# Attention of block 1 and mix of block 2 written as straight lists in a new order

## The reference

```python
# block 1, the attention half of a layer
h = rms_norm(x, ln_attn_g[i])
dq, dk, dv, mq, mk, mv = jnp.split(h @ w_in[i], cuts, axis=-1)
# diff_attention: 4 heads with two maps each, softmax of q k^T * scale + bias(distance), causal
a = p[:, 0] - lam * p[:, 1]
out = rms_norm(einsum('bhqk,bkhe->bqhe', a, v), sub_g) * (1.0 - lam_init)
# moba_attention: 8 heads of 64, one block of 256 keys: plain causal softmax with bias
x = x + jnp.concatenate([y_diff, y_moba], axis=-1) @ w_out[i]

# block 2, the mix of a layer, between two SwiGLU halves
h = rms_norm_2(x, mix_norm[l])
q, k, v, f_logit, xr, gr, g_attn, g_rnn = jnp.split(h @ w_in[l] + b_in[l], SPLIT_POINTS, axis=-1)
c = jnp.cumsum(jax.nn.log_sigmoid(f_logit), axis=1)      # 8 heads
s = einsum('bhqd,bhkd->bhqk', q, k) * scale + (c_i[..., :, None] - c[:, :, None, :])
y_attn = (softmax(where(mask, s, -inf)) @ v) @ w_o_attn[l]
yr = rg_lru(causal_depthwise_conv(xr), ...) * jax.nn.gelu(gr)
merged = jax.nn.sigmoid(g_attn) * y_attn + jax.nn.sigmoid(g_rnn) * (yr @ w_o_rnn[l])
x = x + merged @ w_out[l]
```

## Time and profile before

| | |
|---|---|
| median of 3 runs | 2027.01 us |
| profiled execution, its own time | 2026.93 us |
| its span | 2025.1 us |
| TensorE matmuls busy | 1923.7 us (95%) |
| VectorE, ScalarE busy | 1204.7 us (59%), 1108.7 us (55%) |
| GpSimd busy | 39.9 us (2%) |
| mean granted TensorE clock | 0.979 of full |
| HBM read | 335.09 MB, 166 GB/s |

### The profile page before, as it was taken

One profiled execution on the slowest core, in us unless ns is written; L12 is line 12 of the kernel. 1 busy time (PEld: TensorE's weight loads), 2 busy tenths in 40 slices (PEclk: granted clock), 3 DMA queues, 4 the chain that ended last, 5 costly groups with the idle time before them and its releaser, 6 DMA issues.

```text
span 2025.1 us, 23105 instructions
## 1 busy us (share of the span) xinstructions
PE 1923.7 (95%) x9234; PEld 1600.6 (79%) x9234; DVE 1204.7 (59%) x1746; ACT 1108.7 (55%) x1588; POOL 39.9 (2%) x70
## 2 busy tenths in 40 slices
PE   6969999987999999999989999999999998999999
PEld 5757888765888888887778878888888877887888
DVE  5655776665776654545865655455455577565544
ACT  5745655664655554447865454445444686545442
POOL 2000000000000000000010000000000001000000
PEclk8989999999999999999999999999999999999999
DMA  7424455534554555553354655555555344455552
GB/s 240 146 83 146 167 187 185 166 128 125 166 189 170 183 187 188 187 166 125 130 178 137 218 176 188 191 178 186 187 187 172 123 142 167 139 192 167 187 187 104
DMA packets 156533, 337.65 MB, mean 167 GB/s; under 512 B 5798, under 2 KB 18555, under 8 KB 155915
## 3 DMA queue, kind: packets, MB, share of 16 engines
q1 hardware_dynamic: 153920, 327.57, 48.6%
q0 software_dynamic: 2048, 8.41, 1.4%
q10 hardware_dynamic: 459, 0.20, 0.0%
HBM read 335.09 MB, written 1.07 MB: 166 GB/s over the span
## 4 chain that ended last, share of the span: by engine, by line
PE 79%; DVE 10%; ACT 8%; issue 2%; DMA 1%; POOL 0%; SPq 0%; DVEq 0%; ACTq 0%; POOLq 0%
PE bank L408 24%; PE bank L410 24%; PE bank L409 24%; DVE w_lo L1396 4%; ACT w_hi L932 2%; ACT tmp L1084 1%; PE bank L569 1%; PE bank L523 1%; PE bank L477 1%; DMA raw<-in_w_in 1%; PE bank L658 1%; DVE gss L1571 1%; PE bank L702 1%; DVE tmp L1596 1%; ACT L1084 1%
## 5 line engine op out<-in xcount | busy, mean ns | idle before, releaser
L1396 DVE TENSOR_TENSOR w_lo<-raw,w_hi 128x1024 fp32r<-128x1024 f32 x620 | 733.4, 1221 | 385.5 <-ACT w_hi L932 378.7
L932 ACT ACTIVATE w_hi<-raw 128x1024 fp32r<-128x1024 f32 x620 | 633.9, 1056 | 276.1 <-PE bank L410 275.6
L408 PE MATMUL bank<-w_hi,r_hi 128*128 128x512 f32 (+1 forms) x1792 | 690.6, 385 | 27.3 <-DVE r_lo L1425 11.4
L410 PE MATMUL bank<-w_hi,r_lo 128*128 128x512 f32 (+1 forms) x1792 | 681.2, 380 | 0.0
L409 PE MATMUL bank<-w_lo,r_hi 128*128 128x512 f32 (+1 forms) x1792 | 681.0, 380 | 0.0
L408 PEld LDWEIGHTS bank<-w_hi,r_hi 128*128 128x128 f32 x1792 | 339.9, 190 | 95.1 <-issue 15.0
L410 PEld LDWEIGHTS bank<-w_hi,r_lo 128*128 128x128 f32 x1792 | 339.5, 189 | 64.6
L409 PEld LDWEIGHTS bank<-w_lo,r_hi 128*128 128x128 f32 x1792 | 340.0, 190 | 60.9
L408 PE MATMUL bank<-w_hi,z_hi 128*128 128x512 f32 x656 | 260.6, 397 | 2.0 <-DVE z_lo L1396 2.0
L410 PE MATMUL bank<-w_hi,z_lo 128*128 128x512 f32 x656 | 256.1, 390 | 0.0
L409 PE MATMUL bank<-w_lo,z_hi 128*128 128x512 f32 x656 | 255.4, 389 | 0.0
(11 more groups left out here) (203 smaller groups left out, 1457.0 us busy)
## 6 DMA issues: line engine op xcount, KB each, us to landing
raw<-in_w_in SPq DMA_DIRECT2D x80, 1024.0 KB, 5.1
raw<-in_w_up SPq DMA_DIRECT2D x44, 1024.0 KB, 5.1
raw<-in_ffn_w_gate SPq DMA_DIRECT2D x44, 1024.0 KB, 5.1
raw<-in_ffn_w_up SPq DMA_DIRECT2D x44, 1024.0 KB, 5.1
raw<-in_ffn_w_down SPq DMA_DIRECT2D x44, 1024.0 KB, 4.9
raw<-in_w_down SPq DMA_DIRECT2D x22, 1024.0 KB, 5.0
raw<-in_w_out SPq DMA_DIRECT2D x16, 1024.0 KB, 5.0
raw<-in_w_o_rnn SPq DMA_DIRECT2D x8, 1024.0 KB, 5.0
```

Of the source, the lines that this page charges most:

```text
L408: pe.matmul(out_, lh, rh, start=start, stop=False, skip_group_check=True)
L410: return pe.matmul(out_, ll, rh, start=False, stop=stop, skip_group_check=True)
L932: A_(w_hi[:, n % NH, :], raw[:, u % NS, HALF * h:HALF * (h + 1)], ACT.Copy).then_inc(hi_ready, 1)
L1396: return V.tensor_tensor(dst, src, hi.bitcast(F32), ALU.subtract)
```

## The change

Three edits, in both layers of each block.

1. Splits are listed by half units (`hi(u, h)`, `lo(u, h)`), projections and products by quarters (`quarter(u, half, n, ...)`), and copies, gates and additions by tile of 128 positions. The hooks are gone: each engine's part of the attention of block 1 and of the mix is one straight list of such calls. The other stages keep their loops.
2. Those lists are in a new order.
3. The sums of the forget gates are made: TensorE multiplies the gates by a triangle (`forget_sums`), ScalarE copies the result (8 rows of 384) into `sums_f`, GpSimd stores it to device memory and loads it back to all 128 partitions (`spread`), adds the causal mask (`masked`), and VectorE's `logits` adds the tile where it added the mask. The decay matmuls and the GpSimd products go. Tiles for heads 0 to 3 lie where the recurrence weights were, so GpSimd clears these again for layer 1.

```diff
             def scores(where, p):
-                if b == 2:
-                    pe.wait_ge(decay_ready, pair_at(where, p) - 8 * LAYERS + 1)
+                if b == 1 and p % 4 == 0:
+                    pe.wait_ge(qk_ready, 8 * l + 4 + p)
+                if b == 2 and p == 0:
+                    pe.wait_ge(f_copied, l + 1)
...
-                    if b == 2:
-                        dc = decay[p % 2]
-                        pe.matmul(s[:, 0:256], tri, dc[:, m, 0:256], start=False, stop=False,
-                                  skip_group_check=True)
-                        pe.matmul(s[:, 0:128], one_u[:, 0:128], dc[:, m, 256:384], start=False, stop=True,
-                                  skip_group_check=True)
...
             def logits(where, p):
+                if where[0] == 2 and p == 0:
+                    dve.wait_ge(lru_done, 4 * where[1] + 4)
...
+                if where[0] == 2:
+                    dve.wait_ge(decay_ready, 3 * where[1] + max(p, 1))
...
                 def forget_logits():
+                    pe.wait_ge(rh_ready, KT * norm_at(where, 1) + KT)
...
+                def forget_sums():
+                    pe.wait_ge(f_ready, l + 1)
+                    pe.wait_ge(lru_gates, 4 * l + 4)
+                    o = bank[C][0:H2, :]
+                    pe.matmul(o[:, 0:256], lf[:, 0:H2], cst[:, K_TRI:K_TRI + 256], start=True, stop=False,
+                              skip_group_check=True)
+                    pe.matmul(o[:, 128:256], lf[:, H2:2 * H2], tri, start=False, stop=True, skip_group_check=True
+                              ).then_inc(f_summed, 1)
...
+                def copy_sums():
+                    act.wait_ge(f_summed, l + 1)
+                    for c, n in ((0, 256), (256, 128)):
+                        last = A_(sums_f[:, c:c + n], bank[C][0:H2, 0:n], ACT.Copy, scale=-1.0)
+                    last.then_inc(f_copied, 1)
...
+                pool.wait_ge(f_copied, l + 1)
+                pool.dma_start(by_key[l], sums_f[:, :]).then_inc(st_by_key, 16)
+                pool.wait_ge(st_by_key, 16 * l + 16)
+                def spread(n, dst, head, heads):
+                    src = bass.AP(by_key.tensor, by_key.offset + (l * H2 + head) * 384, [[0, P], [1, heads * 384]])
+                    pool.dma_start(dst, src).then_inc(ld_decay[n], 16)
+                def masked(n, tile, heads):
+                    pool.wait_ge(ld_decay[n], 16 * l + 16)
+                    tri_mask = mask[:, 128:256].unsqueeze(1).broadcast_to([P, heads, 128])
+                    nc.gpsimd.tensor_tensor(tile[:, :, 128:256], tile[:, :, 128:256], tri_mask, ALU.add)
+                    nc.gpsimd.tensor_tensor(tile[:, :, 256:384], tile[:, :, 256:384], tri_mask, ALU.add
+                                            ).then_inc(decay_ready, 1)
```

More of the change, by code:

```diff
@@ L413, in nothing, with quarter @@
                 pass
[L415 removed]
+            def quarter(u, half, n, banks, oh, ol, ready=None, free=None):
                 def tile(t, kk):
@@ new lines, in _ @@
+                turn_second()
+                part(0, 0)
+                part(0, 1)
+                part(0, 2)
+                part(0, 3)
+                part(1, 0)
+                part(1, 1)
+                part(1, 2)
+                turned(0)
+                part(1, 3)
+                part(2, 0)
+                part(2, 1)
+                turned(1)
+                part(2, 2)
+                part(2, 3)
+                part(3, 0)
+                scores(where, 0)
+                part(3, 1)
@@ new lines, in _ @@
+                part(3, 2)
+                turned(2)
+                part(3, 3)
+                scores(where, 1)
+                part(4, 0)
+                turn(where, 0)
+                part(4, 1)
+                scores(where, 2)
+                part(4, 2)
+                turn(where, 1)
+                part(4, 3)
+                turned(3)
+                scores(where, 3)
+                part(5, 0)
+                part(5, 1)
+                turn(where, 2)
+                scores(where, 4)
@@ new lines, in _ @@
+                part(7, 2)
+                part(7, 3)
+                part(8, 0)
+                part(8, 1)
+                part(8, 2)
+                forget_sums()
+                part(8, 3)
+                turned(6)
+                part(9, 0)
+                part(9, 1)
+                part(9, 2)
+                part(9, 3)
+                turned(7)
+                gate_part(0, 0)
+                scores(where, 0)
+                gate_part(0, 1)
+                gate_part(0, 2)
+                gate_part(0, 3)
@@ new lines, in _ @@
+                lo(u0 + 7, 0)
+                lo(u0 + 7, 1)
+                sums(2)
+                logits(where, 0)
+                scale(2)
+                lo(u0 + 8, 0)
+                lo(u0 + 8, 1)
+                lo(u0 + 9, 0)
+                lo(u0 + 9, 1)
+                normalise(where, 0)
+                logits(where, 1)
+                lo(u0 + 10, 0)
+                sums(3)
+                normalise(where, 1)
+                lo(u0 + 10, 1)
+                scale(3)
+                logits(where, 2)
@@ new lines, in _ @@
+                logits(where, 1)
+                lo(u + 24, 0)
+                normalise(where, 1)
+                lo(u + 24, 1)
+                lo(u + 25, 0)
+                gated(0, 0)
+                lo(u + 25, 1)
+                gated(0, 1)
+                att_low(where, 1)
+                lo(u + 26, 0)
+                lo(u + 26, 1)
+                logits(where, 2)
+                normalise(where, 2)
+                lo(u + 27, 0)
+                lo(u + 27, 1)
+                gate(1, 0)
@@ new lines, in _ @@
+                gate(1, 1)
+                att_low(where, 2)
+                logits(where, 3)
+                lo(u + 28, 0)
+                normalise(where, 3)
+                gated(1, 0)
+                lo(u + 28, 1)
+                lo(u + 29, 0)
+                lo(u + 29, 1)
+                lo(u + 30, 0)
+                lo(u + 30, 1)
+                lo(u + 31, 0)
+                gate(2, 0)
+                att_low(where, 3)
+                gated(1, 1)
+                lo(u + 31, 1)
```

1204 lines of the change are left out of this document (704 added, 500 removed).

## The result

The changed kernel takes 1952.89 us (median of 4 runs, 1950.9 to 1953.02), the kernel before 2026.84 (2025.88 to 2028.18) on the same chip: a ratio of 0.963, 95% interval 0.9619 to 0.9642, or 74 us less. The prediction said 49.6 less, with a range from 1960 to 2006. The direction and most places were right; the gain is half as large again. The profiled execution took 1950.9, its span is 1949.1, against 2025.1 before: 76.0 less.

A forecast was written before the change was run, and what follows sets the result against it. TensorE, 79% of the chain, was taken to bound the kernel through idle time, low clock and own instructions; block 1's 32.8 and the mix's 16.8 made 49.6 us off 2026.9: forecast 1977, range 1960 to 2006 (own range 1967 to 1990).

The forecast's parts named there:

- chunk 5: Block 1, up to the end of chunk 5: ends at 107.6 instead of 118.3, gain 10.7 us per layer.
- to the first output quarter: Block 1, from chunk 5's end to the first output quarter: 10.1 instead of 12.2 us, gain 2.0 per layer.
- four early output quarters: Block 1: 17.9 instead of 22.5 us, as copies, exponentials and low parts stand ahead of splits; gain 4.6 per layer.
- to the FFN: Block 1's exit: transposes of x move behind the last quarter, their wait of 0.9 goes; net gain 0.9 us per layer.
- clock of block 1: Block 1: two waits of about 2 us may lower TensorE's clock; 2 us taken back per layer.
- entry of the mix: Block 2: forget products wait for all tiles, 4.1 us lost idle, and run at half clock, 2.3 lost, per layer.
- rest of the mix: Block 2, per layer: gains of 6.3, 1.5, 2.7, 4.7 and 0.9 us; losses of 0.3 (merge) and 1 (GpSimd's path).
- GpSimd's 1: Mix: storing, loading and masking the gate sums takes 12 to 17 us; 1 us lost per layer, bounds 0 and 4.
- rival with tight lists: Each queue runs 2 to 3 us late at four places per mix layer, 1 at five of block 1: near 2005; chance 0.22.
- bound of 4 behind it: Mix entry: lower bound of minus 4 us, half clock for 3.4 us of the first chunk more than before.
- decay products' 6.3: Mix: decay products of 8 heads removed, 7.0 us, two gate-sum products added, 0.7; net gain 6.3 per layer.
- nearly all idle goes: Forget products at full clock, small waits vanish in block 1 and elsewhere: 14 us less, 1963; chance 0.12.

The follow-up runs named there:

- two gap versions: Changed kernel with VectorE normalising block 1's pair 3 later, behind split halves, so TensorE idles some 2.4 or 4.8 us more per layer: 1962.23 and 1966.63 us.
- first version with 12: Against the version with two pieces of 24: forget products in four pieces of 12, each behind a quarter of chunks 0 and 1: 1937.74 us.

## Why the prediction was too small

Its steps, layer 0, against the two traces (gains in us; a stretch runs between the same two instructions in both, before less after):

| step | predicted | measured | how |
|---|---|---|---|
| chunk 5 | 10.7 | 11.8 | 27.75 less 15.95; the 1.3 late start did not come |
| to the first output quarter | 2.0 | 3.9 | 12.12 less 8.19 |
| four early output quarters | 4.6 | 4.8 | 22.49 less 17.68 |
| to the FFN | 0.9 | 2.9 | 16.05 less 13.16 |
| clock of block 1 | -2 | in the above | no fall |
| entry of the mix | -6.4 | -9.0 | 26.16 less 35.17 |
| rest of the mix | 14.8 | 24.7 | 263.85 less 239.14 |

Block 1: 16.2 predicted, 23.4 measured (layer 1: 21.3). Mix: 8.4 predicted, 15.7 in either layer. Twice the mix and both layers of block 1 make 76.1, which is the difference of the spans.

**Two steps failed: the idle time of the walked lists, and the clock.** In layer 0 of block 1, 7.2 us are missing.

- 3.2 lie in the first three steps. The prediction has lengths of 17.0, 10.1 and 17.9 there and waits of 8.3 in them; measured are 41.8 us in all, with 4.4 idle. So 3.9 us of waits did not come. The busy time was right to 0.7: the walk counted at full clock (36.7, measured 37.4), and so it had already counted what the low clock of the earlier trace rows cost.
- 2.0 are the term for the clock: "The clock fell after such gaps before ... I take 2 us back". No fall came in the profiled execution.
- 2.0 lie in the step to the FFN. The prediction had no clock for this stretch. In the kernel before, a fall began right behind the last gap, and the late output quarters ran 3.4 us at half clock, 1.7 lost.

In each layer of the mix 7.3 us are missing. Idle time is the largest part: behind the entry 12.2 went (14.7 less 2.5) and 8.0 were booked, 4.2 more, most of it in the projections. Half clock in the same stretch cost the kernel before 5.6 us (11.2 us of TensorE's busy time, by half) and 1.5 was booked, 4.1 more: the clock of 0.97 and 0.98 in the earlier trace rows was not read as money. But 2.4 of these 5.6 lie right behind the forget products, and the new entry pays them again: it lost 2.6 more than booked, 2.9 by the clock less 0.3 of idle. Over the whole mix of layer 0, kernel before and changed kernel, the clock gave nothing back:

```profile
883.66:1173.67 290.01, 273.99 (x1287) 228.46 (x1286) 180.61 (x276) 179.68 (x268) 13.33 (x22) 0.97 0.48 160
```

```profile
840.10:1114.40 274.30, 266.69 (x1239) 221.96 (x1239) 180.92 (x278) 179.77 (x271) 15.42 (x18) 0.97 0.51 170
```

GpSimd's 1, which was not lost, and 0.6 that I could not trace to an instruction make up the 7.3.

That old order and low clock go together is shown by the version with block 1's old lists, and that gaps bring half clock by the two gap versions. That a given gap brings a fall is not certain, and the 2 us that did not come were in part luck. Ten traces here have block 1's lists as changed, the changed kernel's included; in four of them, of which the version with the late forget products is one, the clock falls in layer 0 behind the short waits that the prediction meant, to 0.89 over 106.6 to 122, a loss of 1.7 us:

```profile
106.60:122.00 15.40, 12.46 (x87) 9.43 (x86) 11.64 (x36) 12.38 (x31) 0.00 (x0) 1.00 0.16 62
```

```profile
106.60:122.00 15.40, 12.45 (x80) 9.29 (x79) 10.04 (x35) 11.05 (x29) 0.00 (x0) 0.89 0.14 53
```

**The waits that did not come.** Chunk 5 started with no delay, not 1.3 late. Waits of 1.9, 2.1 and 0.8 before the first output quarter measured 0.38, 0.45 and 1.45, with 0.43 of issue. In the projections 4.5 us of idle were foreseen and 1.05 came (copying v); in the attention 0.7 and none. The two largest, 0.8 and 2.7 for stores behind gate activations, are zero, though only just: the last store of its chunk ends when TensorE wants it.

```profile
971.87 0.68 ACT L1452 ACTIVATE qk<-bank,par 128x512 f32<-128x512 f32 x1
```

```profile
972.60 0.44 PE L631 MATMUL bank<-cst,stage 128*128 128x128 f32 x2
```

The late entry did not pay for this: with the entry 8 us shorter the projections show no new wait. Where in the walk the 2.7 us were lost I did not settle, so this largest of the missing waits is without a cause. The rival with tight lists was thus the wrong way round.

**What held.** The entry, to the point: 5.3 us of idle foreseen, 5.1 measured; forget products 10.2, measured 10.3. Of the bound of 4 behind it (half clock reaching into the first chunk) 2.8 came: the 9.0 of the entry less 3.8 of idle and 2.4 of forget products. By the likeliest value it was put at nothing. The decay products' 6.3 and the order of the waits that go were right, and so was the early quarters' 4.6. GpSimd's path, -1, cost nothing: of the walk's 12 to 17 us it took 12.7.

Of the 26.5 us that the prediction lacks against the spans, 7.2 and 4.7 lie in block 1's two layers and 7.3 in each layer of the mix. By cause, leaving out the 4.7 of layer 1, which I did not take apart: 12.9 are idle time that went and was not booked (3.9 in block 1, 4.5 in each mix), 6.1 the clock (3.7 in block 1, 1.2 in each mix) and 2 GpSimd. The rival "nearly all idle goes" came nearest, at 1963, but for reasons that did not hold: it had the entry's forget products at full clock, and just these stayed at half. (Its 3.7 per entry is less than the 4.7 that the prediction's own 10.2 and 5.5 give.)

## What to carry to other kernels

Price a gap of TensorE as its length plus what the granted clock loses around it, and take that from the clock column of the stretches *behind* the gap too: when a change removes the gap, both can come back, and they are counted once, either by walking with full-clock durations or by a term of its own. When lists are rewritten for one stage, look at what now stands first in TensorE's list at the entry: 48 narrow products that needed all tiles cost 15 us more there than one chunk later, and cutting them into four pieces, none later than the gates' chain bears, gave 10 more with v's earlier copy.

## What the runs showed of the hardware

- The load of 768 KB took 7.0 us from issue to the first mask beside a stream of weights (318 GB/s in that stretch). In the version with four loads the last took 4.0, where the other engines stood still and no weights moved (second row: no busy time but GpSimd's, and 192 GB/s), and the third 7.0, with VectorE and ScalarE just as idle but weights moving and TensorE mostly at work (first row). So it is the weights' traffic, not VectorE's splits, that goes with the 3 us more. The Trainium skill (DMA: Bandwidth & Descriptors, "Anatomy of one DMA") gave 3.8 in the prediction: the load by itself agrees, the loads beside the weights do not.

```profile
992.76:999.73 6.97, 5.72 (x26) 4.40 (x24) 0.00 (x0) 0.00 (x0) 0.53 (x2) 1.00 0.76 269
```

```profile
999.70:1003.80 4.10, 0.00 (x0) 0.00 (x0) 0.00 (x0) 0.00 (x0) 0.57 (x2) 0.63 0.48 192
```

```profile
999.73 0.53 POOL L403 DMA_DIRECT2D big<-by_key  x1 [6.44 <-DMA big<-by_key]
1003.76 1.26 POOL L409 TENSOR_TENSOR big<-big,cst 128x512 f32<-128x512 f32 x1 [3.50 <-DMA big<-by_key]
1004.99 1.25 POOL L410 TENSOR_TENSOR big<-big,cst 128x512 f32<-128x512 f32 x1
```

- The same two masks took 1.26 and 1.25 us there, with VectorE idle, and 1.50 and 2.25 beside VectorE's splits in the changed kernel. VectorE lost as well: its two splits, elsewhere 2.35 together, took 3.46 (row below). The first split runs 1.2 us, to about 983.5; the first mask, begun at 983.19, ends at 984.7; the second split, begun at 983.46, ends 2.3 us later, near 985.8; the second mask ends at 986.9, 1.1 behind it. So they ran in turn, each held for as long as the other had still to run. The rule of the Trainium skill that the prediction cited (SBUF — State Buffer, "SBUF: two separate sides") says just this, and the trace agrees.

```profile
982.32 3.46 DVE L1653 TENSOR_TENSOR w_lo<-raw,w_hi 128x1024 fp32r<-128x1024 f32 x2 [0.53 <-ACT w_hi L1066]
```

- The clock fell on a run of 48 forget products with no wait directly ahead of it (the last, of 1.3 us, ended 12 to 15 us earlier), both before and in the version with late forget products. With 24 and 24 it fell behind them, with 12 at a time not in layer 0 (0.91, 0.91, 1.00 and 1.00 over the same stretch for 48, 24 and 24, and the two versions with 12). In layer 1 the first version with 12 had one fall, at a wait of 1.8; the same wait in layer 0 had none.
